# Panels: combining and gating on GpSimd instead of VectorE, and steps 1, 2, 4 and 5 of eight in the seven-product form instead of 1, 3 and 5

## What is computed

```python
u = rms_norm(x, norm_g) @ w_in                      # first kind, twice
gate_all = gates.reshape(B, S, N_BRANCH, D_MODEL)   # the last 4 x 2048 columns of u
for n, (y, z) in enumerate(branches):
    branch = y * silu(z)
    merged = merged + sigmoid(gate_all[:, :, n]) * (branch @ w_branch[n])
x = x + merged @ w_out
...
gt, up = split(rms_norm_2(x, g_ffn) @ w_gate_up, 2) # second kind, D_FF = 5632
return x + (silu(gt) * up) @ w_down
```

## Time and profile before

| | us |
|---|---|
| median of 3 runs (3271.31 to 3272.82) | 3272.59 |
| the profiled execution, its time | 3272.8 |
| its span, first to last instruction | 3271.0 |
| TensorE busy | 3258.1 |
| VectorE busy | 2203.4 |
| ScalarE busy | 1638.9 |
| GpSimd busy | 321.3 |
| SyncE queue: bytes moved, mean rate | 619.77 MB, 189 GB/s |

### The profile page before, as it was taken

One profiled execution on the slowest core, in us unless ns is written; L12 is line 12 of the kernel. 1 busy time (PEld: TensorE's weight loads), 2 busy tenths in 40 slices (PEclk: granted clock), 3 DMA queues, 4 the chain that ended last, 5 costly groups with the idle time before them and its releaser, 6 DMA issues.

```text
span 3271.0 us, 39924 instructions
## 1 busy us (share of the span) xinstructions
PE 3258.1 (100%) x15091; PEld 2699.7 (83%) x15091; DVE 2203.4 (67%) x2476; ACT 1638.9 (50%) x2085; POOL 321.3 (10%) x282
## 2 busy tenths in 40 slices
PE   8999999999999999999999999999999999999999
PEld 7888888888888888888888888888888888888887
DVE  5466655588865656555888655575555578888887
ACT  6444445455544444454555445455444455555554
POOL 0111241100000102411000011160000100000000
PEclk9999999999999999999999999999999999999999
DMA  8665565666666655556665675554565656556655
GB/s 300 191 185 166 165 177 162 188 206 193 217 193 205 182 167 166 173 164 186 202 211 183 208 226 170 172 179 144 193 192 183 186 187 204 187 194 204 194 193 180
DMA packets 303808, 619.77 MB, mean 189 GB/s; under 512 B 24961, under 2 KB 29441, under 8 KB 302465
## 3 DMA queue, kind: packets, MB, share of 16 engines
q1 hardware_dynamic: 303616, 617.22, 60.9%
HBM read 609.80 MB, written 7.34 MB: 189 GB/s over the span
## 4 chain that ended last, share of the span: by engine, by line
PE 100%; DMA 0%; DVE 0%; ACT 0%; SPq 0%; issue 0%
PE G L1127 69%; PE X L1048 6%; PE X L1046 6%; PE X L1047 6%; PE X L826 2%; PE G L1048 2%; PE G L1047 2%; PE G L1046 2%; PE X L942 1%; PE X L914 1%; PE G L1121 1%; PE X L969 0%; PE X L968 0%; PE X L935 0%; PE X L916 0%; PE X L889 0%
## 5 line engine op out<-in xcount | busy, mean ns | idle before, releaser
L1452 DVE TENSOR_TENSOR w_lo<-raw,w_hi 128x1024 fp32r<-128x1024 f32 (+1 forms) x1016 | 1236.9, 1223 | 942.2 <-ACT w_hi L1148 915.4
L1148 ACT ACTIVATE w_hi<-raw 128x1024 fp32r<-128x1024 f32 (+1 forms) x1016 | 1052.8, 1041 | 1265.3 <-PE G L1127 1129.0
L1127 PE MATMUL G<-w_hi,xh 128*128 128x512 f32 x1984 | 796.0, 401 | 0.0
L1127 PE MATMUL G<-w_hi,xl 128*128 128x512 f32 x1984 | 775.0, 391 | 0.0
L1127 PE MATMUL G<-w_lo,xh 128*128 128x512 f32 x1984 | 772.7, 389 | 0.0
L1127 PE MATMUL G<-w_hi,yh 128*128 128x512 f32 x1256 | 499.3, 398 | 8.5 <-DVE w_lo L1452 8.5
L1127 PE MATMUL G<-w_hi,yl 128*128 128x512 f32 x1256 | 491.2, 391 | 0.0
L1127 PE MATMUL G<-w_lo,yh 128*128 128x512 f32 x1256 | 490.0, 390 | 0.0
L1127 PEld LDWEIGHTS G<-w_hi,xl 128*128 128x128 f32 x1984 | 372.3, 188 | 81.0
L1127 PEld LDWEIGHTS G<-w_hi,xh 128*128 128x128 f32 x1984 | 372.9, 188 | 73.9 <-issue 2.7
L1127 PEld LDWEIGHTS G<-w_lo,xh 128*128 128x128 f32 x1984 | 373.3, 188 | 72.2
(11 more groups left out here) (261 smaller groups left out, 3164.3 us busy)
## 6 DMA issues: line engine op xcount, KB each, us to landing
raw<-in_w_in SPq DMA_DIRECT2D x572, 512.0 KB, 3.6
raw<-in_w_gate_up SPq DMA_DIRECT2D x176, 512.0 KB, 4.1
raw<-in_w_down SPq DMA_DIRECT2D x88, 512.0 KB, 4.5
raw<-in_w_out SPq DMA_DIRECT2D x64, 512.0 KB, 4.2
raw_more<-in_w_in SPq DMA_DIRECT2D x52, 512.0 KB, 4.4
raw<-in_w_branch SPq DMA_DIRECT2D x48, 512.0 KB, 3.8
raw<-in_w_mem_kv SPq DMA_DIRECT2D x32, 512.0 KB, 6.3
raw<-in_w_o SPq DMA_DIRECT2D x32, 512.0 KB, 3.6
```

The lines of the kernel that those rows point to most:

```text
L1127: mm = M.matmul(G[blk.g][:, t, :], a[:, blk.kk + k, tok], ringed(w, blk, c)[:, j, :], start=(k == 0 and q == 0), stop=(k == blk.kt - 1 and ...
L1148: A(high_of(c)[:, 0:size_of(c)], source_of(c), ACT.Copy).then_inc(hi_done, 1)
L1452: V.tensor_tensor(low_of(c)[:, 0:n], source_of(c), high_of(c)[:, 0:n].bitcast(F32), ALU.subtract).then_inc(lo_done, 1)
```

## The change

`SEVEN` becomes (1, 2, 4, 5). `cross` and `silu_product` move from VectorE's program to GpSimd's. GpSimd has no per-token scale in its products, so ScalarE applies it ahead, in two more passes over `sig_wide` behind a wait for its own sigmoids.

```diff
-SEVEN = (1, 3, 5)
+SEVEN = (1, 2, 4, 5)
...
@@ ScalarE, wide_sigmoid(b)
                 if b in FF_PANEL:
                     for t in range(TT):
                         last = A(hidden[:, t, :], sig_wide[:, t, 0:NB], ACT.Sigmoid, scale=by[:, t:t + 1])
+                    last.then_inc(gate_read, 1)
+                    act.wait_ge(gate_read, FF_PANEL[b] + 1)
+                    for t in range(TT):
+                        last = A(sig_wide[:, t, :], sig_wide[:, t, :], ACT.Copy, scale=by[:, t:t + 1])
                     last.then_inc(wide_sig, 1)
...
@@ VectorE, loop over units (cross and silu_product with their bodies leave)
-                    if e - 2 in STEM_ENDS:
-                        cross(STEM_ENDS[e - 2])
-                    if e - 2 in ENDS and ENDS[e - 2] in FF_PANEL:
-                        silu_product(ENDS[e - 2])
...
@@ GpSimd
+            def cross(b):
+
+                freed(pool, b)
+                link(V.tensor_tensor(six, sig_wide[:, 0, 0:NB], six, ALU.add))
+                V.tensor_tensor(sig_wide[:, 0, NB:], six, five, ALU.add)
+                link(V.tensor_tensor(sig_wide[:, 1, 0:NB], six, sig_wide[:, 1, 0:NB], ALU.add))
+                V.tensor_tensor(sig_wide[:, 1, NB:], sig_wide[:, 1, 0:NB], five, ALU.add).then_inc(crossed, 1)
+
+            def silu_product(b):
+
+                pool.wait_ge(wide_sig, PANEL_N[b] + 1)
+                link(V.tensor_tensor(hidden, sig_wide[:, :, 0:NB], hidden, ALU.mult))
+                V.tensor_tensor(hidden, sig_wide[:, :, NB:], hidden, ALU.mult).then_inc(hidden_ready, 1)
...
+                for b in PANELS:
+                    if BLOCKS[b].name[1] == l:
+                        cross(b)
...
+            for b in FF_PANEL:
+                cross(b)
+                silu_product(b)
```

More of the change, by code:

```diff
@@ L587, in hybrid_program @@
         sums_done, forms_ready, forms_done, form_rounded = sem("sums_done"), sem("forms_ready"), sem("forms_done"), sem("form_rounded")
-        crossed, x_banks_free, wide_sig, hidden_ready = sem("crossed"), sem("x_banks_free"), sem("wide_sig"), sem("hidden_ready")
+        crossed, x_banks_free, wide_sig, gate_read, hidden_ready = sem("crossed"), sem("x_banks_free"), sem("wide_sig"), sem("gate_read"), sem("hidden_ready")
         hi_done, lo_done, mm_done = sem("hi_done"), sem("lo_done"), sem("mm_done")
@@ L1452, in split @@
                 V.tensor_tensor(low_of(c)[:, 0:n], source_of(c), high_of(c)[:, 0:n].bitcast(F32), ALU.subtract).then_inc(lo_done, 1)
[L1454 to L1460, removed]
             def gather(b):
@@ L1469, in gather @@
                     V.tensor_tensor(sig_wide[:, t, :], both, sig_wide[:, t, :], ALU.add).then_inc(x_banks_free, 1)
[L1471 to L1481, removed]
             def scaled_product(b, dst, by, other):
```

## The result

The changed kernel takes **3319.38 us** (median of 4 runs, 3316.33 to 3321.01); the kernel before, measured beside it, 3272.28 us. The ratio is 1.0143, with an interval of 1.0126 to 1.0161: 1.4% slower. The direction was forecast, the size was not: 3282.9 us, at most 3297. The profiled execution took 3318.89 us.

The account below looks back on a forecast made before the run. TensorE was taken to bound the kernel. Matmuls -11.6, stops between neighbouring steps +21.3 and the fourth form +0.4 gave +10.1 us on the profiled 3272.8: 3282.9 us, range 3274 to 3297.

Parts of the forecast that it names:

- What bounds the kernel: Whole kernel: TensorE, busy 3258.1 of 3271.0 us, sets the time; a matmul less saves time if others keep ahead.
- matmuls -11.6: One more seven-product step in each of 19 panels takes away 57 matmuls: -11.6 us.
- Two steps in a row, +21.3: Feed-forward panels: neighbouring seven-product steps stop TensorE 0.96 us in the first pair, 1.41 in the second; +21.3 us over nine panels.
- the 0.19 of the upper bound: Stops between neighbouring steps: another 0.19 us for refilling TensorE, 3.4 us more in all, as the upper bound.
- the slot rule: Feed-forward part: four slots fix the start of VectorE's `sums24` split, leaving 1.03 us of lead however little VectorE does.
- Merge stage, nothing: Ten panels of the first two layers: six slots keep VectorE's lead at about 2 us or more, so neighbours cost nothing.
- The fourth form, +0.4: Form for the added step, made late ahead of the first feed-forward panel: 0.4 us with the handover, once.
- Behind them waits the copy for a unit that TensorE wants 14 us after the end. Nothing.: ScalarE behind a feed-forward panel: two scaling passes of 1.06 us each delay only this copy, at no cost.
- GpSimd: `cross`, nothing: Combining moved to GpSimd: its additions end in time for VectorE's gather, by 1.4 us at worst, so no cost.
- the products, nothing: GpSimd behind a feed-forward panel: products end 12.3 us after it, TensorE's transpose asks at 13.60; no cost.
- rival 3: GpSimd's products meet VectorE splits and end at 14.7; TensorE stands 1.2 us more a panel: +10.8, 3293.7 us; chance 0.15.
- The clock stays 1.000: Sign that the forecast is right: TensorE's granted clock stays 1.000 in the changed kernel.

Follow-up runs that it names:

- experiment 2: Here its run with the four seven-product steps and only `cross` moved to GpSimd, products on VectorE, no scaling passes, against the kernel before: 3287.12 us (1.0045).
- experiment 3: Changed kernel with VectorE's add of the first `down` block moved ahead of the split of the sixth unit: 3298.68 us, 1.0083 against the kernel before.

## Why the prediction was wrong

- **What bounds the kernel; matmuls -11.6.** Right. Every stop of VectorE's or GpSimd's showed in TensorE's chain at once.
- **Two steps in a row, +21.3.** Right in size: a period with the four steps alone is 66.15 us, forecast 66.2. Its split was wrong. Both pairs of a panel cost the same, 1.1 to 1.2 us (on PE 0.11 + 0.43 + 0.11 + 0.33 + 0.11 in the first): the first more than the 0.96, since the refilling that the forecast left out is there (0.11 us between the first two matmuls behind each stop; the 0.19 of the upper bound is in no run), the second less than 1.41. There VectorE did wait for its load (0.9 us ahead of L1438 at 2819.10, 0.7 in the run with the four steps alone), but its `sums24` split began no later than the slot allowed: in that run it still waited 0.16 us for ScalarE's copy. Two errors cancelled, which is luck. That the slot rule is the cause is shown by the runs with six slots.
- **Merge stage, nothing.** Wrong by 3.2 us: the ten panels gained 2.87 where they should give 6.1. The cover inside the panels held. The stops are behind each layer's last panel (3.1 us on PE, two times), which the forecast did not follow to its end: VectorE's `gather` stands behind a split that waits for a load. Chain of the run with four steps in the layers and everything on VectorE:

```profile
891.49 11.46 DMA raw<-in_w_out
...
905.21 2.36 DVE gates L1470 x2
907.62 0.66 PE X L827 x4
```

- **The fourth form, +0.4.** It cost 1.2 us; one unit earlier, it cost nothing.
- **ScalarE: "Behind them waits the copy for a unit that TensorE wants 14 us after the end. Nothing."** This is the step that failed. The copy was named rightly, and its unit is wanted at 13.6. But behind the split of that unit, in VectorE's own order, stands the add that frees a bank, and TensorE wants the bank at 10.9. I asked who wants the late operation's result, and not what stands behind it on the engine that waits for it. Passes alone: +10.4 us, measured. The larger part of the miss is in the next step but one, and it goes through the same add.
- **GpSimd: `cross`, nothing.** Right (experiment 2).
- **GpSimd: the products, nothing, with rival 3 at 0.15.** The trace before showed a split and a GpSimd operation holding each other up, and I priced only what that does to the product. The split is held up as well, 1.23 to 2.60 us, and that goes onto the same add: from the passes alone to the whole move it is +24.7 us, about half of it the clock. Rival 3's own working was nearly right: both products meet a split and end at 14.7, it said; they ended 14.3 after the panel's end (2785.65 + 3.26 - 2774.62), and TensorE stands 0.7 to 1.0 us for them once the bank is out of the way. The rule of the Trainium skill (SBUF — State Buffer, "Who interferes with whom"), that such operations of VectorE and GpSimd exclude each other for a whole instruction, is borne out in both directions; I had written that the sum was the same without it, and it is not.
- **The clock stays 1.000.** Wrong: 0.998. No row of the kernel before had a stop behind which it could fall.

Put together from the measured terms, the sum is 3282.9 + 34.2 (nine panels at 5.56 in place of 1.76) + 1.7 (3.2 behind the layers' last panels, less the 1.5 by which this execution was ahead before the first panel) + 0.8 (the fourth form) = 3319.6 us, against 3318.9 profiled.

## What to carry to other kernels

When an operation becomes late, list what stands behind it in the order of every engine that waits for it, and look in that list for releases of banks and buffers: they are wanted earlier than any result. Check the two engines on either side of a move: an operation put on GpSimd beside VectorE's can cost VectorE time, also where GpSimd has time to spare (here some 50 of 75 us came back). Whether that matters depends on what waits for the lengthened instruction: moving `cross` cost nothing in sum. And when a stop is removed, look for the next wait a microsecond or two behind it before its whole length is counted as gain; here 40% of it came back (20.7 us won where 34 were counted on).

## What the runs showed of the hardware that was not expected

- A single stop of 2.1 to 3.0 us in an engine that is otherwise fully busy was enough for TensorE's clock to fall to its lower level behind it, in 21 of 27 panels (changed kernel 4 of 9, the move alone 8 of 9, the changed kernel with six slots 9 of 9). Behind stops of 1.0 us (up to 1.6) it fell in none of 18. These counts are of the profiled executions; four other executions of the two kernels with stops of 1.0 us list a clock of 0.999, so it seems to fall now and then there too. In experiment 3 it fell behind the one stop of 2.2 us and behind none of the eight near 1 us. The length alone does not decide: the changed kernel has the longest of these stops and the fewest falls. Each fall costs some 1.5 us, on top of the stop.
- GpSimd and VectorE lengthen each other: GpSimd's products of 128x1024, 1.90 us alone, took 2.42 and 3.26; VectorE's split beside them 2.60 for 1.23, and two of them 3.42 to 4.58 for 2.35.
- The same matmuls with two more weight slots in use ran at 13.72 us for 60 instead of 13.60, at full clock and with no wait. Its cause stays open.
